# Second block of a two-block network on one core: where four weight splits stand in the queues of ScalarE and VectorE, and how the norms sum their squares

## The chip, the cores and the metric

One Trainium2 chip, one of its cores. The metric is the device time of one launch in microseconds. TensorE (PE) multiplies matrices, VectorE (DVE) and ScalarE (ACT) work on rows, GpSimd (POOL) and SyncE (SP, here the DMA queue) help. Each engine runs its own program in order; semaphores tie the programs together.

## The reference, cut to what matters

Two blocks of two layers follow one another. The change touches the second block alone. For each of its layers, on 256 tokens of x and, in layer 0 only, 256 more of a context, all with 1024 channels:

```python
h = x * (1 + sc1) + sh1
y = token_mixers(h, ...)          # 4 heads A (window, sink), 4 heads B, 8 heads C (MLA); y = concat(heads) @ w_out
x = layer_norm(ALPHA * x + g1 * y, ln1_g, ln1_b)
h = x * (1 + sc2) + sh2
x = layer_norm(ALPHA * x + g2 * ((relu(h @ w_fc1) ** 2) @ w_fc2), ln2_g, ln2_b)

def layer_norm(x, g, b):
    mu = mean(x); var = mean((x - mu) ** 2)
    return (x - mu) * rsqrt(var + EPS) * g + b
```

So a layer has one attention and two layer norms; the block has two attentions and four norms.

## The kernel before

Rows are kept transposed: channels on the 128 partitions (8 tiles `XX[:, k]`), tokens along the free axis. Layer 0 works on n = 512 columns (x and context), layer 1 on n = 256.

**Weights.** All weights come through a ring of 2048-column slots, 1 MB each, in the order of one plan; SyncE issues a load (L2669) as soon as the last reader of that slot has signalled. Products are made of two halves: a weight chunk is *split* into a high part, which ScalarE writes by a copy to the rounded type (`Ffn.split_act`, L2321 to L2327), and a low part, which VectorE writes as the difference, back into the ring slot (`Ffn.split_dve`, L2329 to L2333). TensorE then makes three products per tile (`mm3`, L297 to L299) and waits for "low". Chunk i of a feed-forward stage uses buffer i % 3, so chunk i waits for the use of chunk i - 3. Chunks 0 to 3 are the output weights w_out, 4 and 5 the first two of w_fc1.

**Attention** (`Mix`, L1685). After projections, norms and rotations each engine loops over pairs of units; a unit is 128 queries of one head. Per step i, TensorE (L1951) makes the scores of pair i, the transposes of pair i - 1 (L1983) and the products with values of pair i - 2 (L2006). VectorE (L2233) takes the maxima of pair i (L2268, L2270; heads A first get a mask or a copy, L2261, L2262), copies the output of pair i - 2 (L2240) and normalises pair i (L2246, L2248). ScalarE (L2075) does the exponentials of pair i (L2104, L2106), then copies the transposes of pair i - 1 out of their bank (L2085). There are two banks for transposes, so the transposes of a pair wait for the copies of the pair before. Pairs 0 and 1 are heads A, 2 and 3 heads B, 4 to 7 heads C, and then the next 128 queries start with heads A again; layer 0 has 32 pairs, layer 1 has 16. Ahead of this loop ScalarE splits chunks 0 and 1 (L2073, L2074) and VectorE follows (L2231, L2232).

**Feed-forward stage** (`Ffn`, L2274). TensorE makes the 8 output tiles (two for each of the chunks 0 to 3), and sums the new rows by a product with a matrix of ones (`pe_sum`, L2354). Behind tiles 1, 3, 5 and 7 ScalarE and VectorE split chunks 2, 3, 4 and 5 (L2450, L2534). Then comes the first norm (v = 0):

- VectorE: mean (L2499), 8 centred rows (L2502), later the reciprocal (L2504);
- ScalarE: 8 squares into `dev` (L2432), later the root (L2434);
- TensorE (`pe_norm`, L2340): 8 products with ones, one for each square as it comes (L2345).

In layer 0 a memset of bank 7 (`bg.begin`, L2537) stands between the split of chunk 5 and the mean; it opens the work on the next layer's modulation. The second norm (v = 1) is the same behind the last w_fc2 tile, with no split or memset before it.

Of the kernel before, what the change touches and what calls it, by code (L numbers as in the profile page):

```python
# [205 lines left out]
def build(nc, d):  # L206
    plan, freed = [], []

    with ExitStack() as ctx:
# [28 lines left out]
        XX = k8(XXt[:, :], 512)  # L238
# [1446 lines left out]
        class Mix:  # L1685
# [365 lines left out]
            def act(self, act):  # L2051
                st, NQ = self.st, self.n
                for ev in self.events:
                    if ev[0] == "proj":
                        if ev[3] == 1:
                            self.split_act(act, ev[2] + 3)
                    elif ev[0] == "part":
                        self.act_part(act, *ev[1:])
                    elif ev[0] == "uq":
                        h = ev[1]  # L2060
                        st.wait_ge(act, "uq", h)
                        act.activation(self.qC[0:96, h, 0:NQ], bank[self.ro.of["uq", h][0]][0:96, 0:NQ], ACT.Copy,
                                       scale=96.0 ** -0.5).then_inc(st.act("evicted", ("uq", h)), 1)
                    elif ev[0] == "uk" and ev[1] % 2 == 0:
                        h = ev[1]
                        st.wait_ge(act, "uk", h)
                        act.activation(self.kC[0:64, h, :], bank[self.ro.of["uk", h][0]][0:64, :], ACT.Copy).then_inc(st.act("evicted", ("uk", h)), 1)
                    elif ev[0] == "uv":
                        i = ev[1]
                        st.wait_ge(act, "uv", i)  # L2070
                        act.activation(self.vC[:, i, :], bank[self.ro.of["uv", i][0]][:, :], ACT.Copy).then_inc(st.act("evicted", ("uv", i)), 1)
                self.scratch_free(act)
                self.ffn.split_act(act, 0)  # L2073
                self.ffn.split_act(act, 1)  # L2074
                for i in range(len(self.units) // 2 + 1):  # L2075
                    for u in self.pair(i):
                        self.act_rest(act, u)
                    for u in self.pair(i):
                        self.act_exp(act, u)
                    for u in self.pair(i - 1):  # L2080
                        n = self.heads(u)[2]
                        st.wait_ge(act, "turned", u)
                        if u >= 4:
                            st.wait_ge(act, "o", u // 2 * 2 - 4)
                        act.activation(self.pT[u % 4][:, 0:n], bank[self.T.of["t", u][0]][:, 0:n], ACT.Copy).then_inc(st.act("evicted", ("t", u)), 1)  # L2085
# [116 lines left out]
            def dve(self, dve):  # L2202
# [25 lines left out]
                        dve.tensor_tensor(self.qC[rr, h:h + 2, 0:256], a1, a2, ADD).then_inc(st.dve("qrope", h), 1)  # L2228
                        st.at["scratch", ("rot", h)] = st.at["qrope", h]
                self.scratch_free(dve)  # L2230
                self.ffn.split_dve(dve, 0)  # L2231
                self.ffn.split_dve(dve, 1)  # L2232
                for i in range(len(self.units) // 2 + 2):  # L2233
                    for u in self.pair(i):
                        self.dve_most(dve, u)
                    if i >= 2:
# [37 lines left out]
        class Ffn:  # L2274
# [65 lines left out]
            def pe_norm(self, pe, v):  # L2340
                st, n = self.st, self.n
                b = bank_of(pe, st, self.ro, "var", v)
                for k in range(8):
                    st.wait_ge(pe, "dev", v, k)
                    t = pe.matmul(b[:, 0:n], ones, self.dev[:, k, 0:n], start=k == 0, stop=k == 7)  # L2345
                t.then_inc(st.pe("var", v), 1)

            def pe_sum(self, pe, v, o):
# [79 lines left out]
            def act_norm(self, act, v):  # L2428
                st, n = self.st, self.n
                for k in range(8):  # L2430
                    st.wait_ge(act, "centred", v, k)
                    act.activation(self.dev[:, k, 0:n], XX[:, k, 0:n], ACT.Square).then_inc(st.act("dev", v, k), 1)  # L2432
                st.wait_ge(act, "var", v)
                act.activation(self.mu[:, 0:n], bank[self.ro.of["var", v][0]][:, 0:n], ACT.Sqrt, scale=1.0 / 1024, bias=EPS).then_inc(st.act("evicted", ("var", v)), 1)  # L2434

            def act(self, act):
# [5 lines left out]
                for o in range(8):  # L2442
# [4 lines left out]
                        c = slice(256 * q, 256 * q + 256)  # L2447
                        t = act.activation(self.tmp[o % 2][:, c], bank[self.ro.of["out", o][0]][:, c], ACT.Copy, scale=mod[:, 16 + o, q:q + 1])
                    t.then_inc(st.act("evicted", ("out", o)), 1)
                    if o % 2:  # L2450
                        self.split_act(act, 2 + o // 2)
                self.act_norm(act, 0)
                s = 0
# [42 lines left out]
            def dve_norm(self, dve, v):  # L2496
# [3 lines left out]
                st.wait_ge(dve, "mu", v)  # L2500
                for k in range(8):
                    dve.tensor_tensor(XX[:, k, 0:n], XX[:, k, 0:n], self.mu[:, 0:n], SUB).then_inc(st.dve("centred", v, k), 1)  # L2502
                st.wait_ge(dve, "evicted", ("var", v))
                dve.reciprocal(self.rs[:, 0:n], self.mu[:, 0:n]).then_inc(st.dve("rs", v), 1)  # L2504
                st.wait_ge(dve, "rs", v)
# [19 lines left out]
            def dve(self, dve):  # L2525
# [5 lines left out]
                for o in range(8):  # L2531
                    st.wait_ge(dve, "evicted", ("out", o))
                    dve.scalar_tensor_tensor(out=XX[:, o, 0:n], in0=XX[:, o, 0:n], scalar=ALPHA, in1=self.tmp[o % 2][:, 0:n], op0=MUL, op1=ADD).then_inc(st.dve("res", 0, o), 1)
                    if o % 2:  # L2534
                        self.split_dve(dve, 2 + o // 2)
                if not self.last:
                    self.bg.begin(dve)  # L2537
                self.dve_norm(dve, 0)
                st.wait_ge(dve, "gh")
                for k in range(8):  # L2540
# [357 lines left out]
```

## Time and profile before

| | us |
|---|---|
| median of 3 runs | 2104.78 |
| lowest, highest | 2096.36, 2105.37 |
| the profiled execution | 2100.62 |
| its span in the trace | 2098.8 |
| busy in the span: PE, DVE, ACT, POOL | 1906.4, 1019.7, 756.9, 112.6 |

The profile is of one execution. Times of rows are microseconds from the start of its span. A row of a timeline merges like instructions that follow one another ("x8"), the second number being the time from the first one's start to the last one's end.
### The profile page before, as it was taken

To read this page: it belongs to the slowest core of one execution; us is meant where nothing else is said; L and a number is where in the kernel's file an instruction comes from. 1 tells how busy PE (TensorE), PEld (TensorE's weight loads), DVE (VectorE), ACT (ScalarE), POOL (GpSimd) and SP (SyncE) were. 2 spreads that over 40 slices of the span, in tenths; PEclk is the share of its full clock that TensorE was granted. 3 is DMA by queue.
4 is the path that set the end of the run, shared out by engine and by line. 5 is a ranking of instruction groups with operands and counts; after the bars stand their busy time and mean duration, and the time that the engine had idled before them with its cause. 6 is when DMAs were issued, how large, how long until landed. Compare 5 with 4: busy or idle time off the path is not lost.

```text
span 2098.8 us, 24684 instructions
## 1 busy us (share of the span) xinstructions
PE 1906.4 (91%) x10104; PEld 1331.0 (63%) x10104; DVE 1019.7 (49%) x1676; ACT 756.9 (36%) x1200; POOL 112.6 (5%) x152
## 2 busy tenths in 40 slices
PE   6988799999898999999979879999999897988997
PEld 3654555555575555557535646777777573578997
DVE  1483532323445323256467554444444665655665
ACT  1154243423242434243256434222222323644433
POOL 0590000000000000000000011000000100010000
PEclk9999899999999999999979989999999897989999
DMA  9668499999556999992200112435344131024430
GB/s 393 249 253 323 158 403 400 409 407 365 221 210 250 371 416 421 421 374 80 81 21 1 40 41 94 187 123 191 148 158 183 40 121 40 1 81 159 180 144 21
DMA packets 61705, 429.14 MB, mean 204 GB/s; under 512 B 6544, under 2 KB 9744, under 8 KB 9872
## 3 DMA queue, kind: packets, MB, share of 16 engines
q1 hardware_dynamic: 61584, 427.46, 51.6%
q8 instruction: 84, 1.38, 0.3%
q14 instruction: 37, 0.30, 0.0%
HBM read 426.38 MB, written 1.05 MB: 204 GB/s over the span
## 4 chain that ended last, share of the span: by engine, by line
PE 76%; DVE 13%; ACT 8%; issue 1%; DMA 1%; SPq 0%; DVEq 0%; POOL 0%; ACTq 0%
PE bank L293 15%; PE bank L297 11%; PE bank L299 10%; PE bank L298 10%; PE bank L1008 10%; PE bank L996 7%; PE bank L332 3%; DVE ring_halves L2333 2%; ACT work_halves L2327 2%; PE bank L2006 2%; ACT work_halves L928 2%; PE bank L1983 2%; DVE ring_halves L935 2%; PE bank L2345 1%; DMA ring<-in_ws_dram 1%
## 5 line engine op out<-in xcount | busy, mean ns | idle before, releaser
L297 PE MATMUL bank<-work_halves 128*128 128x512 f32 (+1 forms) x1344 | 475.9, 354 | 35.8 <-DVE ring_halves L2333 10.0
L299 PE MATMUL bank<-work_halves,ring_halves 128*128 128x512 f32 (+1 forms) x1344 | 461.4, 343 | 0.0
L297 PEld LDWEIGHTS bank<-work_halves 128*128 128x128 f32 x1344 | 258.8, 193 | 92.1 <-issue 31.4
L298 PE MATMUL bank<-HH_halves,work_halves 128*128 128x512 f32 (+1 forms) x832 | 289.5, 348 | 0.0
L299 PEld LDWEIGHTS bank<-work_halves,ring_halves 128*128 128x128 f32 x1344 | 258.6, 192 | 29.1
L1008 PE MATMUL bank<-ring,work 128*64 128x512 f32 x1024 | 261.2, 598 | 0.4 <-ACT work_halves L1191 0.4
L2333 DVE TENSOR_TENSOR ring_halves<-ring,work_halves 128x2048 fp32r<-128x2048 f32 x72 | 164.5, 2287 | 54.2 <-ACT work_halves L2327 54.2
L293 PE MATMUL bank<-HH,ring 128*128 128x256 f32 x768 | 176.2, 389 | 16.0 <-DVE HH L473 6.6
L293 PEld LDWEIGHTS bank<-HH,ring 128*128 128x128 f32 x768 | 148.3, 195 | 49.3 <-issue 18.7
L298 PEld LDWEIGHTS bank<-HH_halves,work_halves 128*128 128x128 f32 x832 | 161.9, 195 | 20.0 <-issue 2.2
L298 PE MATMUL bank<-work_halves 128*128 128x512 f32 (+1 forms) x512 | 172.1, 336 | 0.0
L2327 ACT ACTIVATE work_halves<-ring 128x2048 fp32r<-128x2048 f32 x72 | 135.6, 1904 | 63.7 <-PE bank L299 47.7
L1008 PEld LDWEIGHTS bank<-ring,work 128*64 128x64 f32 x1024 | 76.3, 136 | 121.2 <-issue 116.0
L996 PE MATMUL bank<-work_halves 128*128 128x512 f32 x400 | 133.6, 408 | 9.3 <-DVE ring_halves L935 6.7
L935 DVE TENSOR_TENSOR ring_halves<-ring,work_halves 128x2048 fp32r<-128x2048 f32 x44 | 99.0, 2287 | 83.9 <-ACT work_halves L928 83.9
L2594 DVE SCALAR_TENSOR_TENSOR XX<-bank,modt,XX 128x256 f32<-128x256 f32 x192 | 83.5, 478 | 93.8 <-PE bank L299 93.0
L332 PE MATMUL bank<-ring,condt 128*1 128x512 f32 (+1 forms) x744 | 98.1, 625 | 20.9 <-DMA ring<-in_ws_dram 16.6
L2487 ACT ACTIVATE work<-bank 128x512 f32<-128x512 f32 (+1 forms) x64 | 31.0, 485 | 235.4 <-PE bank L299 235.4
L298 PEld LDWEIGHTS bank<-work_halves 128*128 128x128 f32 x512 | 97.1, 190 | 10.8 <-issue 1.2
L996 PEld LDWEIGHTS bank<-work_halves 128*128 128x128 f32 x400 | 76.8, 193 | 29.7 <-DVE ring_halves L935 9.6
L2581 DVE TENSOR_TENSOR work<-work 128x512 f32<-128x512 f32 (+1 forms) x64 | 35.6, 556 | 108.8 <-ACT work L2487 108.8
L1303 DVE TENSOR_TENSOR work<-work,bank 128x512 f32<-128x512 f32 x20 | 13.7, 685 | 149.3 <-PE bank L1008 97.5
(302 smaller groups left out, 2567.8 us busy)
## 6 DMA issues: line engine op xcount, KB each, us to landing
ring<-in_ws_dram SPq DMA_DIRECT2D x380, 1024.0 KB, 7.3
work<-in_ws_dram SPq DMA_DIRECT2D x23, 1024.0 KB, 9.3
con<-in_con_dram SPq DMA_DIRECT2D x1, 1204.0 KB, 15.7
XX<-in_xT_dram SPq DMA_DIRECT2D x1, 1024.0 KB, 11.9
XX<-in_cT_dram SPq DMA_DIRECT2D x1, 1024.0 KB, 15.3
out_dram<-XX SPq DMA_DIRECT2D x1, 1024.0 KB, 4.8
par<-in_par_dram SPq DMA_DIRECT2D x1, 338.0 KB, 3.0
con<-in_con_dram SPq DMA_DIRECT2D x1, 128.0 KB, 2.9
```

The source lines that it names most:

```text
L293: t = pe.matmul(out, l, r, start=i == 0, stop=i == len(pairs) - 1)
L297: pe.matmul(out, l[0], r[0], start=start, stop=False)
L298: pe.matmul(out, l[0], r[1], start=False, stop=False)
L299: return pe.matmul(out, l[1], r[0], start=False, stop=stop)
L332: m = pe.matmul(bank[7][32 * t:32 * t + n, :], c, ring_of(key)[:, 512 * t:512 * t + 512], start=False, stop=k == 7, skip_group_check=True)
L928: act.activation(self.high_of(i), k8(ring_of(key), 256), ACT.Copy).then_inc(st.act("high", i), 1)
L935: dve.tensor_tensor(k8(r_(w), 256), k8(w, 256), self.high_of(i).bitcast(F32), SUB).then_inc(st.dve("low", i), 1)
L996: m = pe.matmul(k8(b[:, :], 256), left[x][:, k, :], right[y][:, 2 * k:2 * k + 2, :], start=first and k == x == y == 0, stop=last and k == ...
L1008: m = pe.matmul(b[c, :], left[:, k, c], ring_of(self.w[i])[:, 512 * k:512 * k + 512], start=first and k == 0, stop=last and k == 3, skip_g ...
L2327: act.activation(r_(self.buf[i % 3]), ring_of(self.w[i]), ACT.Copy).then_inc(st.act("high", i), 1)
L2333: dve.tensor_tensor(r_(ring_of(self.w[i])), ring_of(self.w[i]), r_(self.buf[i % 3]).bitcast(F32), SUB).then_inc(st.dve("low", i), 1)
L2594: t = dve.scalar_tensor_tensor(out=XX[:, o, c], in0=bank[self.ro.of["fc2", f, o][0]][:, c], scalar=mod[:, 40 + o, q:q + 1], in1=XX[:, o, c ...
```

## The change

Three edits, all in the second block.

1. The splits of chunks 0 and 1 leave the place ahead of the attention loop. ScalarE makes them inside the loop, ahead of steps 3 and 5; VectorE ahead of steps 4 and 6.
2. The split of chunk 5 leaves the place behind output tile 7. ScalarE makes it behind the eight squares of the first norm, VectorE behind the additions of edit 3; the memset follows it.
3. In all four norms VectorE adds the squares in pairs (four additions, behind the eight centred rows), and TensorE makes four products with ones instead of eight.

```diff
@@ -2070,9 +2070,9 @@
                         st.wait_ge(act, "uv", i)
                         act.activation(self.vC[:, i, :], bank[self.ro.of["uv", i][0]][:, :], ACT.Copy).then_inc(st.act("evicted", ("uv", i)), 1)
                 self.scratch_free(act)
-                self.ffn.split_act(act, 0)
-                self.ffn.split_act(act, 1)
                 for i in range(len(self.units) // 2 + 1):
+                    if i in (3, 5):
+                        self.ffn.split_act(act, i // 4)
                     for u in self.pair(i):
                         self.act_rest(act, u)
                     for u in self.pair(i):
@@ -2228,9 +2228,9 @@
                         dve.tensor_tensor(self.qC[rr, h:h + 2, 0:256], a1, a2, ADD).then_inc(st.dve("qrope", h), 1)
                         st.at["scratch", ("rot", h)] = st.at["qrope", h]
                 self.scratch_free(dve)
-                self.ffn.split_dve(dve, 0)
-                self.ffn.split_dve(dve, 1)
                 for i in range(len(self.units) // 2 + 2):
+                    if i in (4, 6):
+                        self.ffn.split_dve(dve, i // 5)
                     for u in self.pair(i):
                         self.dve_most(dve, u)
                     if i >= 2:
@@ -2340,9 +2340,9 @@
             def pe_norm(self, pe, v):
                 st, n = self.st, self.n
                 b = bank_of(pe, st, self.ro, "var", v)
-                for k in range(8):
+                for k in range(0, 8, 2):
                     st.wait_ge(pe, "dev", v, k)
-                    t = pe.matmul(b[:, 0:n], ones, self.dev[:, k, 0:n], start=k == 0, stop=k == 7)
+                    t = pe.matmul(b[:, 0:n], ones, self.dev[:, k, 0:n], start=k == 0, stop=k == 6)
                 t.then_inc(st.pe("var", v), 1)
 
             def pe_sum(self, pe, v, o):
@@ -2429,7 +2429,9 @@
                 st, n = self.st, self.n
                 for k in range(8):
                     st.wait_ge(act, "centred", v, k)
-                    act.activation(self.dev[:, k, 0:n], XX[:, k, 0:n], ACT.Square).then_inc(st.act("dev", v, k), 1)
+                    act.activation(self.dev[:, k, 0:n], XX[:, k, 0:n], ACT.Square).then_inc(st.act("square of", v, k), 1)
+                if v == 0:
+                    self.split_act(act, 5)
                 st.wait_ge(act, "var", v)
                 act.activation(self.mu[:, 0:n], bank[self.ro.of["var", v][0]][:, 0:n], ACT.Sqrt, scale=1.0 / 1024, bias=EPS).then_inc(st.act("evicted", ("var", v)), 1)
 
@@ -2447,7 +2449,7 @@
                         c = slice(256 * q, 256 * q + 256)
                         t = act.activation(self.tmp[o % 2][:, c], bank[self.ro.of["out", o][0]][:, c], ACT.Copy, scale=mod[:, 16 + o, q:q + 1])
                     t.then_inc(st.act("evicted", ("out", o)), 1)
-                    if o % 2:
+                    if o % 2 and o < 7:
                         self.split_act(act, 2 + o // 2)
                 self.act_norm(act, 0)
                 s = 0
@@ -2500,6 +2502,13 @@
                 st.wait_ge(dve, "mu", v)
                 for k in range(8):
                     dve.tensor_tensor(XX[:, k, 0:n], XX[:, k, 0:n], self.mu[:, 0:n], SUB).then_inc(st.dve("centred", v, k), 1)
+                for k in range(0, 8, 2):
+                    st.wait_ge(dve, "square of", v, k + 1)
+                    dve.tensor_tensor(self.dev[:, k, 0:n], self.dev[:, k, 0:n], self.dev[:, k + 1, 0:n], ADD).then_inc(st.dve("dev", v, k), 1)
+                if v == 0:
+                    self.split_dve(dve, 5)
+                    if not self.last:
+                        self.bg.begin(dve)
                 st.wait_ge(dve, "evicted", ("var", v))
                 dve.reciprocal(self.rs[:, 0:n], self.mu[:, 0:n]).then_inc(st.dve("rs", v), 1)
                 st.wait_ge(dve, "rs", v)
@@ -2531,10 +2540,8 @@
                 for o in range(8):
                     st.wait_ge(dve, "evicted", ("out", o))
                     dve.scalar_tensor_tensor(out=XX[:, o, 0:n], in0=XX[:, o, 0:n], scalar=ALPHA, in1=self.tmp[o % 2][:, 0:n], op0=MUL, op1=ADD).then_inc(st.dve("res", 0, o), 1)
-                    if o % 2:
+                    if o % 2 and o < 7:
                         self.split_dve(dve, 2 + o // 2)
-                if not self.last:
-                    self.bg.begin(dve)
                 self.dve_norm(dve, 0)
                 st.wait_ge(dve, "gh")
                 for k in range(8):
```

## Rows read from the trace of the kernel before

**Rows 1.** Page, part 4: the chain that ended last, shares of the span
```profile
PE 76%; DVE 13%; ACT 8%; issue 1%; DMA 1%; SPq 0%; DVEq 0%; POOL 0%; ACTq 0%
```

**Rows 2.** One line's instructions: the weight split, ns min/median/max
```profile
L2327 ACT ACTIVATE work_halves<-ring x72: 1893/1901/1922, 1062.9 to 2060.7; 128x2048 fp32r<-128x2048 f32 x72
...
L2333 DVE TENSOR_TENSOR ring_halves<-ring,work_halves x72: 2278/2291/2295, 1065.0 to 2067.2; 128x2048 fp32r<-128x2048 f32 x72
```

**Rows 3.** Timeline, first attention's start; start us, us, instruction, [idle before <-releaser]
```profile
1062.92 3.71 ACT L2327 ACTIVATE work_halves<-ring 128x2048 fp32r<-128x2048 f32 x2 [8.00 <-DVE work L2228]
...
1069.49 0.29 DVE L2261 TENSOR_TENSOR work<-bank,con 128x128 f32<-128x128 f32 x1
...
1074.92 1.94 PE L1983 MATMUL bank<-con,work 128*128 128x128 f32 x8 [9.11 <-DVE work L2248]
```

**Rows 4.** Timeline, second attention's start
```profile
1761.41 3.71 ACT L2327 ACTIVATE work_halves<-ring 128x2048 fp32r<-128x2048 f32 x2 [8.00 <-DVE work L2228]
...
1767.97 0.29 DVE L2261 TENSOR_TENSOR work<-bank,con 128x128 f32<-128x128 f32 x1
```

**Rows 5.** Timeline, third to fifth pair of heads, one engine after the other
```profile
1085.63 0.69 ACT L2106 ACTIVATE work<-bank,small 128x512 f32<-128x512 f32 x1 [2.46 <-DVE small L2270]
...
1088.95 0.69 ACT L2106 ACTIVATE work<-bank,small 128x512 f32<-128x512 f32 x1 [0.90 <-DVE small L2270]
...
1090.29 1.08 ACT L2085 ACTIVATE work<-bank 128x512 f32<-128x512 f32 x2
...
1088.23 1.28 DVE L2270 TENSOR_REDUCE small<-bank 128x1 f32<-128x512 f32 x2
...
1088.54 1.04 PE L1983 MATMUL bank<-con,work 128*128 128x128 f32 x8
...
1092.36 1.04 PE L1983 MATMUL bank<-con,work 128*128 128x128 f32 x8
```

**Rows 6.** Timeline, first feed-forward stage, norm behind the output projection
```profile
1233.39 0.67 DVE L2499 TENSOR_SCALAR work<-bank 128x512 f32<-128x512 f32 x1
...
1234.10 4.91 DVE L2502 TENSOR_TENSOR XX<-XX,work 128x512 f32<-128x512 f32 x8
...
1235.60 9.29 PE L2345 MATMUL bank<-work,con 128*128 128x512 f32 x16 [4.92 <-ACT work L2432]
...
1244.92 0.60 ACT L2434 ACTIVATE work<-bank 128x512 f32<-128x512 f32 x1 [3.95 <-PE bank L2345]
```

**Rows 7.** Windows: PE, PEld, DVE, ACT, POOL busy, PEclk, DMA share, GB/s
```profile
1235.60:1240.00 4.40, 4.40 (x5) 1.82 (x6) 3.41 (x6) 4.38 (x8) 0.00 (x0) 0.50 0.01 2
...
1869.20:1874.80 5.60, 5.60 (x13) 4.49 (x14) 1.73 (x6) 3.46 (x8) 0.00 (x0) 0.50 0.01 3
```

**Rows 8.** Timeline, the same stage, norm at its end
```profile
1648.77 8.83 PE L2345 MATMUL bank<-work,con 128*128 128x512 f32 x16 [2.24 <-ACT work L2432]
...
1657.63 0.60 ACT L2434 ACTIVATE work<-bank 128x512 f32<-128x512 f32 x1 [4.71 <-PE bank L2345]
```

**Rows 9.** Timeline, second feed-forward stage, norm behind the output projection
```profile
1867.71 0.42 DVE L2499 TENSOR_SCALAR work<-bank 128x256 f32<-128x256 f32 x1
...
1868.16 2.77 DVE L2502 TENSOR_TENSOR XX<-XX,work 128x256 f32<-128x256 f32 x8
...
1869.18 6.50 PE L2345 MATMUL bank<-work,con 128*128 128x256 f32 x16 [4.30 <-ACT work L2432]
...
1876.13 1.75 DVE L2504 RECIPROCAL work<-work 128x256 f32<-128x256 f32 x1 [5.21 <-ACT work L2434]
```

**Rows 10.** Timeline, the kernel's last norm
```profile
2083.07 3.72 PE L2345 MATMUL bank<-work,con 128*128 128x256 f32 x16 [1.42 <-ACT work L2432]
...
2086.83 0.38 ACT L2434 ACTIVATE work<-bank 128x256 f32<-128x256 f32 x1 [1.47 <-PE bank L2345]
```

**Rows 11.** Timeline of ScalarE: a table load and the exponential behind it
```profile
1071.94 1.28 ACT L2104 ACT_TABLE_LOAD   x1
...
1073.24 0.72 ACT L2104 ACTIVATE work<-work,small 128x513 f32<-128x513 f32 x1
```

## The prediction

> **What bounds the kernel now.** I read first the chain that ended last: three quarters of it are TensorE, the rest nearly all VectorE and ScalarE [rows 1]. The change touches no product with weights, so it can only win where TensorE waits. I then read the split of weights by its own instructions: each costs 1.90 us on ScalarE and 2.29 us on VectorE, each time [rows 2]. Third, the timeline at both starts of attention: the last rotation of queries ends, ScalarE splits output chunks 0 and 1, VectorE follows, and only then does VectorE begin the first mask, 6.57 and 6.56 us behind ScalarE's start [rows 3, 4]. TensorE has its scores ready and stands idle 9.11 us. Last, the timeline of the four norms of the two feed-forward stages, where TensorE waits for a mean, centred rows and squares.
>
> All times are of the profiled execution, which took 2100.62 us (span 2098.8); the median of the runs is 2104.78, 4.2 us more. A difference of under 0.5% (10.5 us) is about what a measurement of this kernel can't tell from no change.
>
> **Attention, the gain.** Without the splits VectorE's first mask follows the last rotation at once: 6.6 us earlier in each attention [rows 3, 4] (ScalarE's first row starts 0.1 us behind the rotation; I leave that out). TensorE's scores of pair 0 are done by then: its next work starts behind the masks and exponentials.
>
> **Attention, the cost.** ScalarE now splits ahead of pair 3 and pair 5 of its loop, VectorE ahead of 4 and 6. I follow them through the kernel's own times.
> - ScalarE, pair 3: it is idle 2.46 us before that exponential [rows 5]; 1.90 fits. Cost 0.
> - VectorE, pair 4: the maxima start at 1088.23; behind the split at 1090.52. ScalarE frees the first transpose bank 2.06 + 0.6 us behind the start of the maxima (two exponentials, then the copy at 1090.29, half of 1.08) [rows 5], so at 1093.2. TensorE wanted it at 1092.36 [rows 5]. Cost 0.8.
> - ScalarE, pair 5: its copies end at 1093.65, the split at 1095.5, two exponentials of 1.34 together at 1096.84 (1088.95 to 1090.29 [rows 5]), first bank at 1097.4. TensorE's period is 3.82 us (1088.54 to 1092.36 [rows 5]), so it wants the bank at 1092.36 + 3.82 + 0.8 = 1097.0. Cost 0.4.
> - VectorE, pair 6: the normalised rows of pair 5 end some 0.7 us behind the exponentials, at 1097.6; with the split 1099.9, first bank 2.66 later, 1102.55. TensorE wants it at 1092.36 + 7.63 + 1.2 = 1101.2. Cost 1.3.
> - After that both helpers have slack again in each period (ScalarE was idle 0.90 us before the exponentials of pair 4, more later), so nothing is carried on.
>
> So 2.5 us are paid back, of 8.4 us that the four pieces take. Net 6.6 - 2.5 = 4.1 per attention, **8.2 us for two**. Bounds: nothing paid, 13.2 for two; VectorE's 4.58 and one ScalarE piece of 1.90 paid in full, 0.2. I take the walk through the pairs, since every wait in it has a row. Nobody reads chunks 0 and 1 before the output projection, and their ring slots are freed by that projection as before, so no DMA moves on SyncE's queue; no work of POOL is passed.
>
> **Norms, what changes in each.** Let M be the start of the mean on VectorE. Old: 8 centrings, 8 squares, 8 products with ones, which follow the squares as they come. New: 8 centrings, then 4 additions on VectorE, then 4 products. TensorE starts later and has half the work. The additions are not in the trace; the nearest rows are the centrings, same form, 8 in 4.91 us at 512 columns and 8 in 2.77 at 256 [rows 6, 9].
>
> *Stage 0, first norm (512).* The last split with its memset stands between the sum and the mean. TensorE's idle time of 4.92 us before 1235.60 says that the sum ended at 1230.68; the mean starts at 1233.39 [rows 6]. New M is 1230.8, with 0.1 for the hand-over, 2.6 earlier. First addition from M + 5.6, ends M + 6.3; last ends M + 8.1. Eight half products (the trace counts each product twice) cost 0.855 us each at the lower clock and 0.43 at the higher: the old 16 took 9.29 us, the first 4.4 of them at 0.50 of the clock [rows 6, 7]. The clock stayed low 4.4 and 5.6 us after TensorE began again [rows 7]; with 5.1, six halves at 0.855 and two at 0.43 plus 0.2 of drain are 6.2, end M + 12.5 = 1243.3 against 1244.92. **Gain 1.6**; bounds 0.8 (all at the lower clock, M + 13.3) and 4.9 (additions last, M + 9.2). The displaced split: squares end M + 6.3, ScalarE done M + 8.2, VectorE M + 10.6, memset M + 11.1, all ahead of the root. Cost 0; without that cover up to 4.2.
>
> *Stage 0, second norm (512).* Nothing stood before the mean. Sum ended 2.24 before 1648.77, M = 1646.6; end M + 12.5 = 1659.1 against 1657.63 [rows 8]. **Loss 1.5**; bounds a gain of 1.8 and a loss of 2.3, by the same two clocks.
>
> *Stage 1, first norm (256).* Sum ended 4.30 before 1869.18, at 1864.88; new M 1865.0, old 1867.71 [rows 9]. Products start M + 3.7 (mean 0.45, centrings 2.77, addition 0.42), eight halves at 0.427 (lower clock, kept to 1874.8 before [rows 7]) end M + 7.3, root done M + 7.7. Here the displaced split is about as late: squares end M + 3.7, ScalarE M + 5.6, VectorE M + 7.9. Reciprocal at 1872.9 against 1876.13. **Gain 3.2**; lower bound 2.5.
>
> *Last norm (256).* The old 16 halves took 3.72, at the higher clock throughout, after 1.42 idle [rows 10]. New: M = 2081.7, products start at 2085.4, after 3.8 idle. An idle 2.24 us in stage 0 was enough for the clock to drop: 16 halves there took 8.83 instead of 6.9 [rows 8]. At the lower clock the end is M + 7.3 = 2089.0 against 2086.83. **Loss 2.2**; at the higher clock 0.2.
>
> **Sum:** 8.2 + 1.6 - 1.5 + 3.2 - 2.2 = 9.3 us. 2104.78 - 9.3 = 2095.5 (of the profiled execution: 2091.3).
>
> Two pages bear on this. The table of ScalarE: between exponentials' set and the work before, the load took 1.28 us and the next instruction began 0.02 us behind it [rows 11]. The Trainium skill, "ScalarE: Activation LUTs", What ACT_TABLE_LOAD costs, adds a drain of about 1.38 us to each switch; by that the root of stage 1 would be some 0.8 us later and the sum 8.5 instead of 9.3. The trace shows no such drain, so I don't charge it. The clock: each idle stretch above 2 us named here was followed by slow products [rows 6, 8, 9]. The Trainium skill, "TensorE: Matmul & The Clock Gate", The HAM clock gate, says that the throttled state is the default and activity releases it; that speaks against halving the norms' products, and the trace agrees.
>
> **Rivals.**
> - *The clock rises early.* The idle time before the first transposes falls from 9.1 to 2.5 us [rows 3]; those eight would take 1.04 instead of 1.94 [rows 3, 5], the values behind them save as much, 1.8 per attention; and the last norm keeps its clock, 2.0. Gain 9.3 + 3.6 + 2.0 = 14.9: 2089.9. For it: denser work. Against it: TensorE worked before the old gap too, at the lower clock.
> - *The split is fully paid.* VectorE turns out to be the bound of the pairs; attention wins 0.2 in all, norms 1.1: 2103.5. Against it: the idle times [rows 5].
> - *Something else holds the mean.* If it does not start with the sum, stage 0's first norm loses 1.0, stage 1's wins 0.5: sum 8.2 - 1.0 + 0.5 - 3.7 = 4.0: 2100.8.
> - *Root late.* ScalarE stands for one more table load (1.28) before the root of stage 1: VectorE's reciprocal 0.7 later, 2096.2.
> - *Slower: the clock drops among the heads.* The splits open holes of about 1 us in TensorE's stream; 1.42 us was harmless [rows 10], 2.24 was not [rows 8]. If a hole of some 2 us drops the clock, 5.6 us at half speed cost 2.8; twice per attention, 11.2, and norms at their slow ends (0.8 - 2.3 + 2.5 - 2.2): 8.2 - 1.2 - 11.2 = -4.2: 2109.0.
>
> **Chances.** Forecast 0.50, own range 2092 to 2099; early clock 0.18; fully paid 0.15; held mean 0.08; late root 0.03; slower 0.06. The range 2088 to 2103.5 leaves out the slow case, half of the fully paid one and a fifth of the early clock. Faster by over 0.5% needs 10.5 us: four in ten of the forecast case (my sum is 1.2 short of it), nearly all of the early clock, together 0.38. Slower by over 0.5% is half of the slow case and noise of two others, 0.05. The rest, 0.57, is within.
>
> **What would show it.** Right: first mask directly behind the last rotation; transposes of pair 4 to 6 late by 0.8, 1.2 and 2.5 us in sum and no more after; the mean 0.1 us behind the sum in both first norms; 4 products in about 6 us (512) and 3.4 (256), at 0.5 clock. Wrong: TensorE at the lower clock among the heads, pairs that stay late, or a last norm that still ends within 5.3 us of its mean.

## The result, and the profile after

The changed kernel takes 2088.6 us (median of 20 runs, 2082.16 to 2097.19), the kernel before 2101.28 (20 runs, 2096.15 to 2105.37). The ratio is 0.9939, 95% interval 0.9927 to 0.9950: 12.8 us less, with 10.5 to 15.3. The forecast was 9.3 us less and "within 0.5%"; the time lies inside the range, the gain just across the bound.

The page of the profiled execution (part 1) shows where to look: TensorE is busy 9.2 us less, VectorE 9.7 us more, for 32 fewer records of products and 16 more instructions on VectorE.

```profile
PE 1897.2 (91%) x10072; PEld 1321.8 (63%) x10072; DVE 1029.4 (49%) x1692; ACT 756.5 (36%) x1200; POOL 112.6 (5%) x152
```

The span fell by 11.1 us, from 2098.8 to 2087.7. I cut both traces at the same events: the end of the last rotation of each attention, the first copy of its output, the end of the sum of each norm, its reciprocal, the start of the mean in the second norm of a stage. The stretches in us:

| stretch | before | after | gained | forecast |
|---|---|---|---|---|
| first block, up to the last rotation | 1062.76 | 1064.63 | -1.87 | 0 |
| attention, layer 0 | 115.42 | 109.90 | 5.52 | 4.1 |
| its output projection | 52.49 | 54.09 | -1.60 | 0 |
| first norm, stage 0, sum to reciprocal | 14.88 | 12.37 | 2.51 | 1.6 |
| products of stage 0, to the mean | 401.08 | 400.67 | 0.41 | 0 |
| second norm, stage 0, mean to reciprocal | 11.63 | 12.30 | -0.67 | -1.5 |
| projections of layer 1, to the last rotation | 102.99 | 102.40 | 0.59 | 0 |
| attention, layer 1 | 75.55 | 71.39 | 4.16 | 4.1 |
| its output projection | 28.08 | 28.08 | 0 | 0 |
| first norm, stage 1 | 11.25 | 7.82 | 3.43 | 3.2 |
| products of stage 1 | 205.56 | 205.93 | -0.37 | 0 |
| last norm, mean to reciprocal | 5.56 | 6.56 | -1.00 | -2.2 |
| the rest | 11.55 | 11.56 | 0 | 0 |

The first line holds no edit, and over the fourteen profiled executions of this study it runs from 1060.05 to 1069.86 us. So a single span says little about a few microseconds; below I read stretches from traces and totals from the timed ratios.

**Attention.** The timeline of the changed kernel at the first attention (same columns as [rows 3]):

```profile
1063.95 0.68 DVE L2228 TENSOR_TENSOR work<-work 32x512 f32<-32x512 f32 x1
1064.66 0.29 DVE L2261 TENSOR_TENSOR work<-bank,con 128x128 f32<-128x128 f32 x1
...
1078.30 1.93 ACT L2327 ACTIVATE work_halves<-ring 128x2048 fp32r<-128x2048 f32 x1
...
1082.19 2.28 DVE L2333 TENSOR_TENSOR ring_halves<-ring,work_halves 128x2048 fp32r<-128x2048 f32 x1
```

The last rotation ends at 1064.63, the mask follows at 1064.66, where it used to stand 6.57 us behind ScalarE's start [rows 3]. ScalarE's split of chunk 0 stands at 1078.30 and VectorE's at 1082.19, inside the loop. Now the transposes of pairs 3 to 6 (TensorE alone, same timeline):

```profile
1082.43 1.04 PE L1983 MATMUL bank<-con,work 128*128 128x128 f32 x8
...
1087.10 1.15 PE L1983 MATMUL bank<-con,work 128*128 128x128 f32 x8 [0.69 <-ACT work L2085]
...
1091.21 1.14 PE L1983 MATMUL bank<-con,work 128*128 128x128 f32 x8
...
1096.21 1.15 PE L1983 MATMUL bank<-con,work 128*128 128x128 f32 x8 [0.92 <-ACT work L2085]
```

Their distances are 4.67, 4.11 and 5.00 us. Against a period of 3.82 [rows 5] the pairs come late by 0.85, 0.29 and 1.18, 2.32 in sum; I had worked out 0.8, 0.4 and 1.3. With the pairs behind them the sum grows to 2.4 and stays there.

**Norms.** First norm of stage 0, to be set against [rows 6]:

```profile
1228.66 0.69 DVE L2501 TENSOR_SCALAR work<-bank 128x512 f32<-128x512 f32 x1 [1.22 <-PE bank L2354]
...
1234.21 2.49 DVE L2507 TENSOR_TENSOR work<-work 128x512 f32<-128x512 f32 x4
...
1235.04 5.28 PE L2345 MATMUL bank<-work,con 128*128 128x512 f32 x8 [6.42 <-ACT work L2432]
...
1236.79 2.29 DVE L2333 TENSOR_TENSOR ring_halves<-ring,work_halves 128x2048 fp32r<-128x2048 f32 x1
...
1240.36 0.60 ACT L2436 ACTIVATE work<-bank 128x512 f32<-128x512 f32 x1 [2.30 <-PE bank L2345]
1240.99 3.35 DVE L2513 RECIPROCAL work<-work 128x512 f32<-128x512 f32 x1 [1.31 <-ACT work L2436]
```

The mean starts 0.04 us behind the sum. Four additions of 2.49 us together; the products begin 6.38 us behind the mean and take 5.28 us; the displaced split ends at 1239.08, ahead of the root at 1240.36. The second norm of the stage (against [rows 8]), the first of stage 1 (against [rows 9]) and the last norm (against [rows 10]), one fence for all:

```profile
1647.94 5.35 PE L2345 MATMUL bank<-work,con 128*128 128x512 f32 x8 [6.40 <-DVE work L2507]
...
1859.58 3.62 PE L2345 MATMUL bank<-work,con 128*128 128x256 f32 x8 [3.75 <-ACT work L2432]
1861.36 1.28 ACT L2436 ACT_TABLE_LOAD   x1
1861.38 2.29 DVE L2333 TENSOR_TENSOR ring_halves<-ring,work_halves 128x2048 fp32r<-128x2048 f32 x1 [0.94 <-ACT work_halves L2327]
1863.23 0.38 ACT L2436 ACTIVATE work<-bank 128x256 f32<-128x256 f32 x1 [0.58 <-PE bank L2345]
1863.65 1.75 DVE L2513 RECIPROCAL work<-work 128x256 f32<-128x256 f32 x1
...
2073.20 2.49 PE L2345 MATMUL bank<-work,con 128*128 128x256 f32 x8 [3.66 <-DVE work L2507]
```

Eight half products take 5.35, 3.62 and 2.49 us where sixteen took 8.83, 6.50 and 3.72. In the first norm of stage 1 root and split end within 0.06 us of each other (1863.23 + 0.38 and 1861.38 + 2.29), and the reciprocal follows both without a gap.

### The profile page after: what moved, and what is told of

It reads as the page before. It is cut to its first block, busy times and chain, and to the rows that moved or that the text cites. A ratio compares the mean times of both kernels' runs of the same rounds, so it can differ in the third digit from the quotient of the medians.

```text
span 2087.7 us, 24640 instructions
## 1 busy us (share of the span) xinstructions
PE 1897.2 (91%) x10072; PEld 1321.8 (63%) x10072; DVE 1029.4 (49%) x1692; ACT 756.5 (36%) x1200; POOL 112.6 (5%) x152
## 3 DMA queue, kind: packets, MB, share of 16 engines
q8 instruction: 84, 1.38, 0.3%
## 4 chain that ended last, share of the span: by engine, by line
PE 73%; DVE 15%; ACT 8%; issue 1%; DMA 1%; SPq 0%; DVEq 0%; POOL 0%; ACTq 0%
PE bank L293 14%; PE bank L297 11%; PE bank L299 10%; PE bank L298 10%; PE bank L1008 10%; PE bank L996 7%; PE bank L332 3%; DVE ring_halves L2333 2%; ACT work_halves L2327 2%; ACT work_halves L928 2%; DVE ring_halves L935 2%; DVE work L651 1%; PE bank L2006 1%; PE bank L1983 1%; DMA ring<-in_ws_dram 1%
```

## The experiments

Twelve kernels, each timed 4 to 11 times beside the kernel before. Ratios are against the kernel before; stretches are of one profiled execution each. The diffs of the first three are against the kernel before, the others' against the changed kernel (that of `act_split_in_place` against `pairs_interleaved`).

### The three edits by themselves

`attention_only`: edit 1 alone.

```diff
-                self.ffn.split_act(act, 0)
-                self.ffn.split_act(act, 1)
...
+                    if i in (3, 5):
+                        self.ffn.split_act(act, i // 4)
...
+                    if i in (4, 6):
+                        self.ffn.split_dve(dve, i // 5)
```

> Only the splits of chunks 0 and 1 moved into the attention loop. Walk through the pairs (my theory): from the last rotation to the output projection's first copy 4.1 us less than before in each attention, 5.5 where the clock rises before the first heads C; in all 8.2 to 9.7 us, ratio 0.9953 to 0.9961. Transposes of pairs 4, 5, 6 late by about 0.85, 0.3 and 1.2 us. Rival, the helpers are the bound and the splits are fully paid: under 1 us in all, ratio 0.9995 or more.

Measured: 0.9943, interval 0.9930 to 0.9956. The attentions took 109.95 and 71.35 us, that is 5.5 and 4.2 less, as with all edits together; the projection behind it took 54.11, the same 1.6 more. "Splits fully paid" is out. The ratio is below the 0.9953 to 0.9961 expected; its interval just reaches into them.

`last_split_only`: edit 2 alone, with eight products.

```diff
+                if v == 0:
+                    self.split_act(act, 5)
...
-                    if o % 2:
+                    if o % 2 and o < 7:
...
+                if v == 0:
+                    self.split_dve(dve, 5)
+                    if not self.last:
+                        self.bg.begin(dve)
```

> Only the split of chunk 5 (and the memset) moved behind the squares; eight products with ones as before. My theory: the mean starts 2.6 and 2.7 us earlier in the two first norms and nothing is given back, since in the second stage the sixteen half products end at M + 8.0 and the displaced split at M + 7.9: 5.3 us, ratio 0.9975. Rival, the displaced split now holds the reciprocal: under 3 us, and VectorE idle before the reciprocal is 0 in both norms.

Measured: 0.9957 (0.9944 to 0.9970). Sum to reciprocal went from 14.88 to 11.52 and from 11.25 to 7.76: 6.9 us, more than the 5.3 expected. The timeline of stage 1's norm in this kernel:

```profile
1862.38 3.69 PE L2345 MATMUL bank<-work,con 128*128 128x256 f32 x16 [1.52 <-ACT work L2432]
```

The sixteen half products took 3.69 us, not 6.50: they began after 1.52 us of idle time, not 4.30, and the granted clock stood at 1.00. My expectation had them at the lower clock. But they end 5.17 us behind the mean and the reciprocal starts at 7.73, held by VectorE's own split, which the rival had right. So of the 3.49 us won here 2.79 are the earlier mean, and 0.70 are what the clock and the split together leave. In stage 0 the sixteen took 8.59 us instead of 9.29, which is most of the 0.8 over the 2.6 expected there.

`pairs_only`: edit 3 alone.

```diff
-                for k in range(8):
+                for k in range(0, 8, 2):
...
+                for k in range(0, 8, 2):
+                    st.wait_ge(dve, "square of", v, k + 1)
+                    dve.tensor_tensor(self.dev[:, k, 0:n], self.dev[:, k, 0:n], self.dev[:, k + 1, 0:n], ADD).then_inc(st.dve("dev", v, k), 1)
```

> Only the squares summed in pairs and four products instead of eight, in all four norms. My theory: the products start later and mostly at half clock, so mean to reciprocal changes by +0.2, +0.7, -0.6 and +1.0 us: 1.3 us slower in sum, ratio 1.0006, not told from 1. Rival, half the products is a gain wherever TensorE is waited for: 0.43 to 0.85 us for each product saved, over 6 us in the first stage's two norms, ratio 0.997 or less.

Measured: 0.9998 (0.9987 to 1.0008). The four norms changed by +0.35, +0.70, -0.73 and +1.06 us, sum 1.4. The pairs gain 0.7 us in the first norm of stage 1 and lose more in the other three.

`moves_without_pairs`: edits 1 and 2, that is the changed kernel less edit 3.

> Both moves of splits, eight products as before. My theory: the sum of the two kernels with one move each, 13.5 to 15 us, ratio 0.993 to 0.9936, so the same as the full change within the interval or 1 us better. Rival, the pairs carry part of the full change's gain: ratio over 0.9955.

Measured: 0.9939 (0.9927 to 0.9952), the same as the full change. Its timeline at the first norm of stage 1:

```profile
1856.92 3.69 PE L2345 MATMUL bank<-work,con 128*128 128x256 f32 x16 [1.52 <-ACT work L2432]
...
1860.96 2.29 DVE L2333 TENSOR_TENSOR ring_halves<-ring,work_halves 128x2048 fp32r<-128x2048 f32 x1 [2.29 <-ACT work_halves L2327]
1862.24 0.38 ACT L2436 ACTIVATE work<-bank 128x256 f32<-128x256 f32 x1
1863.17 1.75 DVE L2510 RECIPROCAL work<-work 128x256 f32<-128x256 f32 x1
```

In stage 0 the first norm took 11.73 us (12.37 with pairs), the second 11.64 (12.30), the last norm, in stage 1, 5.56 (6.56). The first norm of stage 1 took 7.76 against 7.82: there the products are long done, and the reciprocal at 1863.17 waits for VectorE's own split (1860.96 + 2.29 = 1863.25, the pipeline's overlap off), not for the root at 1862.24. So with the split displaced, the pairs cost 2.4 us by the stretches, too little for the ratios to show. The stretches of the two moves add up: 9.7 and 6.9, less 1.6 in the projection, are 15.0 by the single kernels and 14.7 in this one. The two timed ratios would add to 12.0 + 9.0 = 21 us where both together gave 12.8; their intervals reach down to 9.2 and 6.3. I go by the stretches; what makes up the rest of that gap was not tried.

### What the pairs wait for

`pairs_interleaved`: the additions behind the centred rows 3, 5 and 7.

```diff
-                for k in range(8):
...
-                for k in range(0, 8, 2):
...
+                for k in (0, 1, 2, 3, "+", 4, 5, "+", 6, 7, "+", "+"):
+                    if k == "+":
+                        st.wait_ge(dve, "square of", v, added + 1)
...
```

> The full change, with the four additions put between the centred rows (behind rows 3, 5 and 7), so that the first sum of two squares is there at M + 3.9 instead of M + 6.3 with 512 columns. My theory: the late start of the products is the cost of the pairs: reciprocal at about M + 10.6 instead of M + 12.3 in both norms of the first stage, M + 5.7 instead of 6.6 in the last norm, but M + 8.5 instead of 7.8 in the second stage's first norm, where squares and split come later. In all 3.5 us less than the full change, ratio 0.992. Rival, the clock alone decides and an earlier start only meets the lower clock longer: under 1 us.

Measured: 0.9939 (0.9925 to 0.9953). The stretches: first norms 12.16 (12.37) and 8.43 (7.82), second 11.20 (12.30), last 6.02 (6.56). So 1.1 and 0.5 us less where no split is near; where one is, 0.2 less and 0.6 more. In all 1.2 us, where I expected 3.5. Its timeline at the first norm of stage 0:

```profile
1233.86 0.69 DVE L2501 TENSOR_SCALAR work<-bank 128x512 f32<-128x512 f32 x1 [1.22 <-PE bank L2354]
...
1237.83 6.57 PE L2345 MATMUL bank<-work,con 128*128 128x512 f32 x8 [4.01 <-ACT work L2432]
...
1243.17 1.28 ACT L2436 ACT_TABLE_LOAD   x1
1243.19 2.29 DVE L2333 TENSOR_TENSOR ring_halves<-ring,work_halves 128x2048 fp32r<-128x2048 f32 x1 [1.11 <-ACT work_halves L2327]
...
1244.47 0.60 ACT L2436 ACTIVATE work<-bank 128x512 f32<-128x512 f32 x1
```

The products start 4.0 us behind the mean instead of 6.4, but take 6.57 us, at a mean granted clock of 0.57; and the split of VectorE (1243.19 to 1245.48, and a memset) ends after the root at 1245.07. Both theories were half right, and the split is a third thing that I had priced only for stage 1. ScalarE's table load ends at 1244.45 here and the root begins at 1244.47: once more no drain between them, where the Trainium skill, "ScalarE: Activation LUTs", What ACT_TABLE_LOAD costs, has about 1.38 us; the measurement decides.

`pe_kept_busy`: the changed kernel, with constant products while TensorE waits. They leave no trace in the result; the true products start the bank anew.

```diff
                 b = bank_of(pe, st, self.ro, "var", v)
+                for _ in range(7 if self.last else 13):
+                    pe.matmul(b[:, 0:256], ones, con_("cos64"), start=True, stop=True)
```

> The full change, and TensorE does products of constants into the bank of the variance while it waits for the first sum (13 of 256 columns in the first stage, 7 in the second; the true products overwrite them). If the lower clock is what makes four products last 5.3 us: granted clock 1.00 at the products, reciprocal at about M + 9.9 instead of M + 12.3 in both norms of the first stage, unchanged (held by the split) in the second stage's first norm, M + 5.7 instead of 6.6 in the last. In all 5.7 us less than the full change, ratio 0.9912. If the clock is not it: nothing, or slower by the constant products.

Measured: 0.9936 (0.9922 to 0.9951), and, in its timeline at the first norm of stage 0:

```profile
1236.33 3.70 PE L2347 MATMUL bank<-work,con 128*128 128x512 f32 x8 [0.71 <-DVE work L2509]
...
1238.17 2.29 DVE L2333 TENSOR_TENSOR ring_halves<-ring,work_halves 128x2048 fp32r<-128x2048 f32 x1
...
1240.06 0.60 ACT L2438 ACTIVATE work<-bank 128x512 f32<-128x512 f32 x1 [0.63 <-PE bank L2347]
...
1240.96 3.29 DVE L2515 RECIPROCAL work<-work 128x512 f32<-128x512 f32 x1
```

Windows of the same kernel and stretch (columns as in [rows 7]):

```profile
1230.00:1234.00 4.00, 4.00 (x21) 3.51 (x20) 3.93 (x7) 2.51 (x5) 0.00 (x0) 1.00 0.36 152
1234.00:1238.00 4.00, 3.29 (x12) 1.94 (x11) 4.00 (x7) 4.00 (x5) 0.00 (x0) 1.00 0.00 2
```

The clock stayed at 1.00 and the eight halves took 3.70 us, not 5.28; they now wait for the additions. First norm 10.96 (12.37), second 10.65 (12.30), last 6.08 (6.56), the first of stage 1 unchanged at 7.76. In all 3.6 us less in the norms, so the clock is what makes four products slow. I had expected 5.7: 9.9 is where the products end, and I had left out the root behind them (0.60); in the first norm the split and the memset held the reciprocal 0.3 us more. The stretches behind them took 0.9 and 1.5 us more and 1.1 less than in the changed kernel, and the timed ratio can't tell 3.6 us from none: it moved by 0.0003 with 0.0015 to either side.

`act_split_in_place`: interleaved additions, ScalarE's half of the split back behind output tile 7.

```diff
-                if v == 0:
-                    self.split_act(act, 5)
...
-                    if o % 2 and o < 7:
+                    if o % 2:
                         self.split_act(act, 2 + o // 2)
```

> The full change with interleaved additions, but ScalarE makes its half of the split of chunk 5 behind output tile 7, as before, where it waits for the mean anyway; VectorE's half stays behind the additions. My theory: with interleaved additions the displaced split holds the reciprocal in both first norms (root done 0.85 us before it). Then sum to reciprocal falls from 12.2 to 11.4 us in the first stage and from 8.4 to 7.2 in the second: 2 us less than with interleaved additions alone, ratio 0.993. Rival, TensorE holds them: unchanged, 0.9939.

Measured: 0.9932 (0.9920 to 0.9944); first norms 11.20 (12.16) and 6.97 (8.43), as expected to 0.2 us; the ratio alone does not tell this kernel from the one before it. ScalarE sat idle between its last copy and the first square, so its half of the split costs nothing there; only VectorE's half had to move.

### The heads

`half_splits`: the four pieces cut in two.

```diff
-                    if i in (3, 5):
-                        self.ffn.split_act(act, i // 4)
+                    for c, part in {3: ((0, 0), (0, 1)), 5: ((1, 0),), 6: ((1, 1),)}.get(i, ()):
+                        self.ffn.half_act(act, c, part)
...
-                    if i in (4, 6):
-                        self.ffn.split_dve(dve, i // 5)
+                    for c, part in {4: ((0, 0),), 5: ((0, 1),), 6: ((1, 0),), 7: ((1, 1),)}.get(i, ()):
+                        self.ffn.half_dve(dve, c, part)
```

> The full change, with the splits inside attention cut into halves of 1024 columns: ScalarE both halves of chunk 0 ahead of step 3, those of chunk 1 ahead of steps 5 and 6, VectorE one half ahead of each of steps 4, 5, 6 and 7. My theory: VectorE is idle 1.14 us and ScalarE 1.39 us in each period of heads C, halves take about 1.2 and 1.05, so the 2.3 us that the transposes of pairs 4 to 6 came late fall to under 0.6 in each attention: 3.5 us less than the full change in all, ratio 0.9922. Rival, every split in the loop costs by its length wherever it stands: unchanged, 0.9939.

Measured: 0.9905 (0.9889 to 0.9921). The timelines of TensorE (transposes of pairs 3 to 7) and of VectorE (one of its halves):

```profile
1077.86 1.04 PE L1983 MATMUL bank<-con,work 128*128 128x128 f32 x8
...
1081.68 1.05 PE L1983 MATMUL bank<-con,work 128*128 128x128 f32 x8
...
1085.52 1.14 PE L1983 MATMUL bank<-con,work 128*128 128x128 f32 x8
...
1089.45 1.15 PE L1983 MATMUL bank<-con,work 128*128 128x128 f32 x8
...
1093.39 1.14 PE L1983 MATMUL bank<-con,work 128*128 128x128 f32 x8 [0.71 <-ACT work L2085]
...
1077.73 1.22 DVE L2329 TENSOR_TENSOR ring_halves<-ring,work_halves 128x1024 fp32r<-128x1024 f32 x1
```

Distances 3.82, 3.84 and 3.93: pairs 4 to 6 are late by 0.13 us in sum instead of 2.32. But VectorE's fourth half stands one step further on, and pair 7 pays for it: its transposes follow 3.94 us behind those of pair 6, where the kernel before has 3.14. The pair behind wins 0.27 back. So the four pieces cost 0.7 us in layer 0, and 0.5 in layer 1 by the same count, instead of 2.4. Attention took 108.17 and 69.46 us (109.90 and 71.39): 3.7 less, 3.5 expected. The projection took 52.47 again, 1.6 less, which I had not expected and which stays open (below). This is the largest step past the change, and its ratio is lower than the 0.9922 expected.

`busy_before_heads`: the changed kernel, with five constant products ahead of the first transposes.

```diff
                     for u in self.pair(i):
                         self.pe_scores(pe, u)
+                    for _ in range(5 if i == 1 else 0):
+                        pe.matmul(bank_of(pe, st, self.T, "t", 0)[:, 0:256], ones, con_("cos64"), start=True, stop=True)
```

> The full change, and TensorE does 5 products of constants into the bank of the first transposes between the scores of pair 1 and those transposes. My theory: attention of layer 0 won 1.4 us more than the walk through the pairs gives because the clock rose before the second transposes, and that of layer 1 did not. With TensorE busy, the second transposes and the first values run at clock 1.00 in both: last rotation to output projection 109.9 us or less in layer 0, and 69.8 instead of 71.4 in layer 1. Ratio 0.9932. If the 1.4 us came from elsewhere: 109.9 and 71.4 as they are.

Measured: 0.9930 (0.9918 to 0.9942). The timeline of TensorE at the second attention, in the changed kernel:

```profile
1761.91 1.94 PE L1983 MATMUL bank<-con,work 128*128 128x128 f32 x8 [2.50 <-DVE work L2248]
...
1766.92 1.97 PE L1983 MATMUL bank<-con,work 128*128 128x128 f32 x8 [1.06 <-ACT work L2085]
1768.82 1.98 PE L2006 MATMUL bank<-work 128*64 128x128 f32 x16
```

The same in `busy_before_heads`:

```profile
1765.19 1.13 PE L1985 MATMUL bank<-con,work 128*128 128x128 f32 x8
...
1768.34 1.14 PE L1985 MATMUL bank<-con,work 128*128 128x128 f32 x8 [0.97 <-ACT work L2087]
1769.41 1.09 PE L2008 MATMUL bank<-work 128*64 128x128 f32 x16
```

Transposes 1.14 instead of 1.97, values 1.09 instead of 1.98, and the stretch is 69.75 instead of 71.39 us; in layer 0 it is 109.92, unchanged. That is the expected pattern: the second transposes and first values of layer 0 already ran at the higher clock in the changed kernel. The ratio alone does not tell the two kernels apart.

### Together

`all_three`: interleaved additions, constant products (8 and 4), half splits.

> Interleaved additions, constant products (8 and 4 of them, since the wait is shorter) and half splits together. By my theory the norms of the first stage reach the reciprocal at M + 9.9, the last at M + 5.7, attention 3.5 us less: 8 to 9 us less than the full change, ratio 0.990. If the gains overlap (the clock), 5 us less.

Measured: 0.9900 (0.9883 to 0.9916).

`best`: the same, ScalarE's split in its old place and the memset back ahead of the mean, where VectorE is idle 1.22 us.

> All three (interleaved additions, constant products in the norms, half splits) with ScalarE's half of the split of chunk 5 in its old place and the memset back ahead of the mean, where VectorE is idle 1.2 us. Sum to reciprocal 12.2 to 10.6 us in the first stage's first norm (held by VectorE's split), 8.4 to 7.2 in the second's; 2.8 us less than the three alone: ratio 0.9887. If the clock falls elsewhere in exchange: 0.990.

Measured: 0.9890 (0.9876 to 0.9903). First norms 10.39 (12.16) and 6.96 (8.43).

`best_busy_heads`: and the constant products ahead of the first transposes.

> The kernel before this one in the list with the constant products ahead of the first transposes added: another 1.4 to 2 us less, ratio 0.988; unchanged if the clock at the first heads is not worth anything.

Measured: 0.9880 (0.9864 to 0.9895), 2075.91 us (median of 4 runs). Layer 1's attention is 67.88 us. It is 25 us faster than the kernel before, twice the gain of the change, and beats both kernels; the last steps each lie within the interval of the one before, the step from the change to this one does not.

## Why the prediction was right, and where it was off

**Bound, and gain at the start of attention.** Right. The first mask follows the last rotation 0.03 us later, and the layer without a change of clock won 4.16 us against 4.1.

**Cost inside the heads.** Right: 0.85, 0.29, 1.18 against 0.8, 0.4, 1.3, and 0.1 after. `half_splits` fits the walk's view that the length of a piece counts against the idle time of a period: the same work, cut in two and spread over more periods, cost 0.5 to 0.7 us instead of 2.4.

**Layer 0's extra 1.4 us.** Not in the sum, and only akin to the rival "the clock rises early". Windows of the changed kernel (columns as in [rows 7]): two in the heads of layer 0, then the products of the first norm, the start of layer 0's output projection, the heads of layer 1 and two in the products of the last norm:

```profile
1070.00:1074.00 4.00, 3.83 (x12) 2.07 (x12) 3.13 (x12) 1.65 (x6) 0.00 (x0) 0.50 0.00 0
1075.00:1087.00 12.00, 11.20 (x84) 6.83 (x84) 10.25 (x23) 9.04 (x21) 0.00 (x0) 1.00 0.01 1
1235.10:1239.00 3.90, 3.90 (x6) 1.74 (x7) 3.81 (x4) 2.94 (x2) 0.00 (x0) 0.59 0.01 2
1174.50:1181.00 6.50, 4.96 (x15) 4.00 (x16) 4.91 (x9) 4.27 (x8) 0.00 (x0) 0.74 0.01 3
...
1762.00:1770.00 8.00, 6.94 (x32) 4.70 (x34) 5.26 (x15) 5.51 (x14) 0.00 (x0) 0.50 0.00 0
2073.20:2074.50 1.30, 1.30 (x6) 1.17 (x7) 0.95 (x3) 0.06 (x1) 0.00 (x0) 1.00 0.00 0
2074.60:2075.70 1.10, 1.09 (x3) 0.34 (x1) 0.00 (x0) 0.00 (x0) 0.00 (x0) 0.50 0.00 0
```

The window of the kernel before at the start of that projection:

```profile
1178.00:1184.00 6.00, 4.32 (x19) 3.60 (x20) 5.06 (x9) 4.28 (x8) 0.00 (x0) 1.00 0.01 3
```

In layer 0 the clock was up from 1075 on, ahead of the second transposes, in layer 1 still at 0.50 up to 1770. `busy_before_heads` shows what such a rise is worth, 1.6 us, by giving it to layer 1. The rival, to which I gave 0.18, asked for more: the first transposes at the higher clock in both layers. They still took 1.94 us in both.

Nor is the early rise shown to come from the shorter idle time. `last_split_only` has the heads of the kernel before and the same 9.11 us of idle time, and its attention in layer 0 took 114.06 us against 115.42. The second transposes, first in the kernel before, then in `last_split_only`:

```profile
1079.93 1.97 PE L1983 MATMUL bank<-con,work 128*128 128x128 f32 x8 [1.07 <-ACT work L2085]
```

```profile
1079.93 1.14 PE L1983 MATMUL bank<-con,work 128*128 128x128 f32 x8 [1.07 <-ACT work L2085]
```

Same start, same wait, other clock. All eleven kernels with moved pieces had the early rise in layer 0, one of the three without had it too. So it is not shown to be a gain of edit 1; what that edit is shown to win is the 4.2 us of layer 1, and about as much in layer 0 (5.5 less the 1.4). What decides the early rise stays open.

**The projection's 1.6 us.** Missing from the sum. TensorE waits 1.86 us ahead of the first output product of layer 0, in all fourteen executions; in the changed kernel the clock was down behind that wait (0.74 over 1174.5 to 1181, where the kernel before had 1.00 at the same place). It is no chance of one execution: 54.1 us in all seven kernels with whole pieces in the heads, 52.5 in all four with halves. But `last_split_only`, whose heads are as before, took 53.9 and `pairs_only` 52.5. So the pieces alone do not decide it, and neither does the length of the wait; no run isolates what does, and it stays open. In these eight (the seven and `last_split_only`) the slow start gave back what the early rise in the same layer had won.

**First norm of stage 0.** Gain 2.51 against 1.6. The step that was off is the length of the products: 5.28 us, worked out as 6.2, since I let the lower clock last 5.1 us; a mean of 0.59 over 1235.1 to 1239.0 makes it 3.2 us. Inside the bounds given. The second norm lost 0.67 against 1.5 for the same term (5.35 against 6.2).

**First norm of stage 1.** Gain 3.43 against 3.2, and held by the split as worked out (7.78 us behind the mean against 7.9). But the pairs have no part in it: `last_split_only` gets 3.49 with all eight products, which ran at the higher clock.

**Last norm.** Loss 1.00 against 2.2: the products took 2.49 us, where I had 3.4 and the lower clock throughout. In spite of the 3.66 us of idle time before them they began at the higher clock: it was 1.00 up to 2074.5 and 0.50 from 2074.6 on. My bound was off too. I put the loss at the higher clock at 0.2; products of the same kind take 2.0 us at 1.00 in `pe_kept_busy`, and the norm lost 0.5 there.

**The sum.** 12.3 us for the stretches of the sum and the projection behind layer 0's attention (5.5 + 4.2 - 1.6 + 2.5 - 0.7 + 3.4 - 1.0) against 9.3. The norms gave 3.2 more than forecast and attention 1.5, the projection took 1.6; all of these but 0.3 us are terms of the clock. That the sum is off by only 3.0 us is partly luck: the 1.4 us that it lacked in layer 0's attention and the 1.6 us that it lacked in the projection behind it cancel. I put 0.57 on "within 0.5%", and it was faster by 0.61%, interval 0.50 to 0.73.

**Rivals.** Fully paid: refuted by `attention_only`. Held mean: refuted, 0.04 us. Late root: the table load at 1861.36 ends before the split does, and the root at 1863.23 was released by TensorE. Slower by the clock among the heads: the holes were 0.69 and 0.92 us and the clock stayed at 1.00.

**Edit 3.** The earlier mean alone was worth 2.6 and 2.7 us in my sum, so the 1.1 I had for all norms put the pairs at a loss of 4.2. They lost 1.4 us alone (0.9998) and 2.4 beside the moves. The change's gain is that of its two moves.

## What to carry to other kernels

A piece of work that stands between a producer and the engine everyone waits for is best moved to where its engine is idle, in pieces about as long as the idle time of one period: VectorE's two pieces of 2.29 us, with ScalarE's two of 1.90, cost 2.4 us in the heads, the same work in halves 0.5 to 0.7. Move each engine's part by itself; in the norms only VectorE's half stood in the way, and ScalarE's was better left. Fewer products were no gain in sum where TensorE waited for their input: the additions that halve them delay the first one, and the products behind the longer pause ran partly at the lower clock.

## What the runs showed that I had not expected

A shorter pause can be worth more than its length: with the last split out of the way, sixteen half products took 3.69 us behind a pause of 1.52 us, where they had taken 6.50 behind 4.30. But a pause's length alone does not tell what follows: behind the same 1.86 us the output projection of layer 0 began at the higher clock in six executions and met the lower one in eight. Constant products in a pause held the clock (1.00 throughout, the real ones 3.70 instead of 5.28 us). And stretches that no edit touches moved: 1060.05 to 1069.86 us for the first block in fourteen executions, 52.5 or 54.1 for one projection.
